# Three always-present slots of split weights in place of four, and three further ones in the MLP in place of two, in a decoder step

## The reference

```
h = rmsnorm(x);  proj = h @ w_in          # 1024 -> 4 x 512: pool channels, q, k, v
A = causal multi-scale pooling of the pool channels, a 128x128 map per group, a gain
B = attention, 8 heads x 64, rotary; decode sequences read 256 paged keys and values
x = x + concat(A, B) @ w_out
x = x + cross_attend(rmsnorm(x), mk, mv, w_cq, w_co)   # 4 heads x 256, 256 memory rows
x = x + square(relu(rmsnorm(x) @ w_up)) @ w_down       # 1024 -> 4096 -> 1024
y = rmsnorm(x)
```

## Time and profile before

| | |
|---|---|
| median of 3 runs | 417.19 us (416.75 to 417.71) |
| the profiled execution's own time | 417.26 us |
| its span in the trace | 415.2 us |
| PE busy | 409.0 us, 99% of the span |
| DVE busy | 253.1 us, 61% |
| ACT busy | 226.7 us, 55% |
| POOL busy | 31.9 us, 8% |
| DMA, mean rate over the span | 233 GB/s |

### The profile page before, as it was taken

The page is one execution under the profiler, slowest core; times in us unless marked ns, Lnnn a source line. Parts: engine busy times, 40 slices in busy tenths (PEclk is TensorE's granted clock), DMA queues, the critical chain, the costliest instruction groups (busy, mean ns, idle before and its releaser), DMA issues.

```text
span 415.2 us, 8425 instructions
## 1 busy us (share of the span) xinstructions
PE 409.0 (99%) x3372; PEld 383.6 (92%) x3372; DVE 253.1 (61%) x400; ACT 226.7 (55%) x392; POOL 31.9 (8%) x41
## 2 busy tenths in 40 slices
PE   8999999999999999999999999999999999999995
PEld 8999979986879998957899999999999999999995
DVE  5899988576254796453259777766667534454302
ACT  5866957925364484424357666666565443453313
POOL 1004026000000120000022000000000000010010
PEclk9999999999999999999999999999999999999999
DMA  8999858974989968995537545655565555545002
GB/s 277 400 385 365 279 205 233 336 275 172 370 313 339 380 228 321 362 394 234 203 103 250 208 135 193 202 181 167 191 202 201 196 174 193 188 162 182 2 2 104
DMA packets 37257, 96.60 MB, mean 233 GB/s; under 512 B 4186, under 2 KB 13274, under 8 KB 37082
## 3 DMA queue, kind: packets, MB, share of 16 engines
q1 hardware_dynamic: 35106, 92.24, 63.5%
q10 hardware_dynamic: 2112, 3.82, 2.5%
HBM read 91.73 MB, written 4.54 MB: 232 GB/s over the span
## 4 chain that ended last, share of the span: by engine, by line
PE 85%; DVE 7%; DMA 4%; SPq 2%; issue 1%; ACT 1%; DVEq 0%
PE psum L1110 70%; PE psum L832 5%; DVE w_lo L1401 2%; PE psum L1052 2%; DMA raw<-in_w_in 2%; PE psum L960 2%; PE psum L947 2%; DMA pages<-in_page_table 1%; DMA raw<-in_w_ck 1%; SPq L778 1%; DVE mix_lo L1405 1%; PE psum L893 1%; PE psum L931 1%; ACT w_hi L1133 1%; PE psum L953 0%
## 5 line engine op out<-in xcount | busy, mean ns | idle before, releaser
L1401 DVE TENSOR_TENSOR w_lo<-raw,w_hi 128x1024 fp32r<-128x1024 f32 x67 | 82.6, 1243 | 61.0 <-ACT w_hi L1133 60.8
L1133 ACT ACTIVATE w_hi<-raw 128x1024 fp32r<-128x1024 f32 (+1 forms) x73 | 73.8, 1019 | 57.8 <-PE psum L1110 41.6
L1110 PE MATMUL psum<-mix_hi,w_hi 128*128 128x264 f32 (+1 forms) x288 | 82.4, 286 | 0.0
L1110 PE MATMUL psum<-mix_hi,w_lo 128*128 128x264 f32 (+1 forms) x288 | 81.1, 282 | 0.0
L1110 PE MATMUL psum<-mix_lo,w_hi 128*128 128x264 f32 (+1 forms) x288 | 81.1, 281 | 0.0
L1110 PE MATMUL psum<-act_hi,w_hi 128*128 128x264 f32 x232 | 66.5, 287 | 0.5 <-DVE w_lo L1401 0.5
L1110 PE MATMUL psum<-act_lo,w_hi 128*128 128x264 f32 x232 | 65.6, 283 | 0.0
L1110 PE MATMUL psum<-act_hi,w_lo 128*128 128x264 f32 x232 | 65.4, 282 | 0.0
L1110 PEld LDWEIGHTS psum<-mix_hi,w_hi 128*128 128x128 f32 x288 | 54.0, 188 | 1.0 <-issue 0.8
L1110 PEld LDWEIGHTS psum<-mix_lo,w_hi 128*128 128x128 f32 x288 | 54.0, 188 | 0.1
L1110 PEld LDWEIGHTS psum<-mix_hi,w_lo 128*128 128x128 f32 x288 | 54.0, 188 | 0.0
(11 more groups left out here) (208 smaller groups left out, 813.9 us busy)
## 6 DMA issues: line engine op xcount, KB each, us to landing
raw<-in_w_down SPq DMA_DIRECT2D x20, 512.0 KB, 3.3
raw<-in_w_up SPq DMA_DIRECT2D x18, 512.0 KB, 3.8
raw_more<-in_w_up SPq DMA_DIRECT2D x14, 512.0 KB, 3.7
stage<-in_mem_v SPq DMA_DIRECT2D x12, 512.0 KB, 6.6
raw_more<-in_w_down SPq DMA_DIRECT2D x12, 512.0 KB, 4.2
stage<-in_cache_v SPq DMA_DIRECT2D x16, 256.0 KB, 6.5
keysT<-in_cache_k SPq DMA_DIRECT2D x16, 256.0 KB, 5.4
keysT<-in_mem_k SPq DMA_DIRECT2D x8, 512.0 KB, 6.9
```

What stands on the lines that cost most here:

```text
L1110: mm = pe.matmul(out, a, b, start=first and m == 0, stop=end_ and m == 2)
L1133: return nc.scalar.activation(out, in_, ACT.Copy, scale=scale)
L1401: V.tensor_tensor(lo_of(c), raw_of(c), hi_of(c).bitcast(F32), ALU.subtract).then_inc(w_lo_ready, 1)
```

## The change

`SPLIT` becomes 3 and `MORE_SPLIT` becomes 3, so that there are six split slots in the MLP as before, and three in place of four up to chunk 55. `AHEAD` follows and becomes 2. Chunk s is then split in turn s-3 until the MLP and waits for chunk s-3. `plan_splits` starts at chunk 3 (`PARTED`), as before in effect: the old start, `AHEAD`, was 3 too. Turn -1, ahead of the loop, has no whole split any more, hence the `.get`: chunk 3 moves into turn 0, chunk 4 into turn 1.

```diff
-SPLIT, MORE_SPLIT = 4, 2
+SPLIT, MORE_SPLIT = 3, 3
 AHEAD = SPLIT - 1
@@ plan_splits
-    for s in range(AHEAD, NC):
+    for s in range(PARTED, NC):
@@ ACT, ahead of its loop
-            for s in SPLITS_AT[0]:
+            for s in SPLITS_AT.get(0, ()):
                 split_hi(s)
```

## The result

The changed kernel takes 422.43 us, the median of four executions (420.7, 422.48, 422.38, 423.3), against 416.97 us for the kernel before on the same chip (four executions, 416.57 to 417.71). The ratio is 1.0124, 95% interval 1.0103 to 1.0144: slower by 1.2%. The forecast was 423.0 us. The profiled execution took 420.7 us, with a span of 418.7 us. The mean granted clock over the span was 1.0 in the profiled execution and 0.948, 0.995 and 0.995 in the three others.

What follows compares the result with a forecast made beforehand. PE's list of matmuls was taken to bound the kernel, busy 409.0 of 415.2 us, so the change could mainly add waits. Six terms summed to 5.8 us on 417.26, giving 423.0 us against the median 417.19; range 419.6 to 427.0.

Steps and rivals of the forecast that it cites:

- Term A: Chunk 4: its low part moves behind the three adds, so PE waits; +1.4 us, between 1.2 and 2.4.
- Terms B and C: Chunks 9 and 13: low parts move behind rotation work; +0.3 us (0 to 1.4) and +0.6 us (0 to 1.6).
- Term D: Prompt scores near 57 us: a moved split may delay DVE emptying their banks; +0.1 us, between -0.2 and +1.1.
- Term E: Chunk 42: split moves behind chunk 39's take-out, and raw loads come later; +2.6 us, between 1.0 and 4.
- the first measure: For each chunk: end of the next chunk's low part before, less the chunk's start on PE before; positive meant lateness.
- rival 1: The loads absorb the shift, joining a backlog and landing when they did; 420.2 us, chance 0.17.
- Term F: From 150 us on: later chunk loads delay decode memory reads sharing SP's queue; +0.8 us, between 0 and 2.2.
- Rival 3: The clock falls to 1.2 GHz behind a wait, one chunk at that level costing 2.9 us; 425.9 us, chance 0.06.
- Rivals 2, 4 and 5: Loads land later and drag PE, 428.2 us, 0.08; nothing changes, 417.2 us, 0.04; faster, 416.5 us, 0.03.

Runs made afterwards that it cites:

- the repeat: The changed kernel run once more, unchanged, for a second trace and more times: 421.01 us, ratio 1.0091.
- five raw slots alone: Changed kernel, three split slots kept, with five raw weight slots from the start in place of three: 418.8 us, ratio 1.004.
- both together: Changed kernel with five raw slots from the start and chunk 4's split put back in its old place: 417.32 us, ratio 1.0014.
- the late places: Kernel before, four and two split slots kept, with splits at the changed kernel's places, one turn later: 418.68 us, ratio 1.0053.
- late loads: Kernel before, four split slots and old split places; loads of chunks 36 to 44 wait for one chunk later's low part: 422.63 us, ratio 1.0124.
- the pair of kernels: Kernel before with loads of chunks 36 to 44 delayed, without and with 20 spare matmuls before chunk 42: 422.63 and 420.57 us.

## Why the prediction was right, and where it was not

The sign and the mechanism held: three slots make PE later at the four chunks named, and nothing changes in the MLP. But that 423.0 us came close to 422.43 us was in good part luck: two errors offset each other. The terms come to 3.4 us in place of 5.8, and the clock, which was a rival, most likely added some 1.5 us to three of the four executions, and late landings some tenths. In the repeat, where one of five executions was of this kind, the median was 421.01 us. For two of the three the mean granted clock of 0.995 says so, the same as in the traced fall of the repeat. The third has 0.948, which would be some 44 us at the lower level (an estimate: 0.052 of 420.4 us, doubled) in an execution that took no longer than the others; this stays unexplained. A trace with the fall was taken of one execution of this kernel only, in the repeat.

**Term A** was right to 0.1 us, and for the reason given: low part 4 ended 0.1 us before the time worked out (18.92 against 19.05). Putting that split back under loads that do not hold it up saves some 1.4 us (five raw slots alone are 1.9 us over the kernel before on the same chip, both together 0.5).

**Terms B and C** were right: +0.15 and +0.70 for 0.3 and 0.6. They are all that remains with both large causes taken away (+0.5 us, interval 0.2 to 1.0). At chunk 9 PE's lateness grows without a marked wait.

**Term D** had the wrong sign. PE does not wait for the bank any more, and the time between chunk 13 and there became 0.44 us shorter, of which the old wait was 0.2. That is outside the range, whose lower end was -0.2. Of the further 0.24 us, 0.18 are gained at the matmuls of L884, at 53.03 us before; the cause was not looked into.

**Term E** is the step that failed in size, +1.6 for +2.6, and its two parts failed differently. The first, 1.0 us for the place of split 42 alone, rested on moving everything around the take-out with PE. The run of the late places with four slots shows 0 there. In the kernel before, DVE's adds were held up by low parts 41 and 42, and those by a landing, and the change takes low part 42 out of their way; so this stretch had room against PE that the first measure, the end of low part s+1 less the start of chunk s, does not see. It sees where a low part ended, not what it had waited for. The second part, the late raw loads, was right in kind. High part 41 came at 144.73 us, where the prediction had 146 for itself and 143.5 for rival 1; it is nearly half way. That the whole step is 1.6 us, as this part was to be, is chance. By the prediction's own count this part is how much more the adds are late than PE: 3.7 - 2.2 there, 2.26 - 1.63 here, 0.6 us. The other 1.0 is the place of split 42 after all, but it costs only where late loads hold the take-out back. The prediction's 2.2 us for PE's lateness ahead of chunk 42 is also not its own sum of A to D, which is 2.4. That the loads are the cause is shown from both sides: five raw slots remove the wait (421.01 to 418.8), and late loads with four split slots make it (417.25 to 422.63). The terms also are not independent. With PE 1.3 us less late the wait grew by 0.7, so that undoing A alone saved 0.9 us (421.01 to 420.14) rather than 1.3.

**Term F** was not there: no wait for a landing near 188 us, and PE's lateness goes from 3.33 at chunk 42 to 3.44 us at the end. PE had fallen as far behind as the loads.

**The rivals.** Rival 1 gave 420.2 us for loads that absorb the shift. In the executions where the clock holds, 420.7 us, the truth lies nearer to it than to the forecast. Rival 3 was given 6% and makes most of the rest. The prediction put against it that the longest wait is 2.6 us; but a wait of 2.14 us was followed by 0.50. Its price in that trace is 1.5 us and not the 2.9 us of one chunk at the lower level, since the stretch ends within the chunk. The executions of 422.4 to 423.3 us lie 1.7 to 2.6 us over the others; later landings may be part of that. With late loads the lower level lasted longer: PE lost 2.7 us from the second wait's end to its last matmul, and the pair of kernels differs by 2.1 us in the median. The Trainium skill (TensorE: Matmul & The Clock Gate, "What's actually happening"), which the prediction named for the fall and the return of the clock, agrees with these traces in kind: 0.50 behind a wait, 1.00 again with PE busy. Rivals 2, 4 and 5 are out: no term reached its upper bound, the waits came, and nothing was won. The waits of PE came to 4.2 us where the prediction looked for about 7.5.

What stays open is what decides whether the clock falls in a given execution. With a wait of 1.53 us and one of 2.23 us it stayed at 1.00; behind one of 2.14 us it fell. In the kernel of the late places alone, two of six executions took 420.2 and 420.4 us against 418.6, without such a wait in the profiled one and with mean granted clocks of 0.997 and 0.998; their cause was not found either.

## What to carry to other kernels

Fewer buffers in a chain of stages cost where something else stands in the written order between two uses, and through the stage that feeds it: here the loss at the far end of the attention came from raw slots being released later, and more raw slots cured it. Before a shift is priced by where an instruction ended, look at what it had waited for: a stretch that itself waits for a landing has room against the engine that seems to set it. A wait of some 2 us in front of a busy TensorE can have a second price behind it, in some executions and not in others. Independent matmuls in the wait took it away with late loads; in the changed kernel no execution with them was slow, but the median was no lower.

## What the runs showed of the hardware

The granted clock fell to 0.50 at waits that the prediction had thought too short to matter: 2.14 us in one execution, and 1.51 and 1.44 us with six matmuls between them in another. PE had been fully busy up to the first wait in both. The stretches ahead of it, in the repeat of the changed kernel and in the kernel with late loads (columns as before):

```profile
141.00:151.00 10.00, 10.00 (x86) 10.00 (x85) 6.61 (x11) 5.04 (x10) 1.79 (x3) 1.00 0.98 374
```

```profile
130.00:148.80 18.80, 18.80 (x158) 18.68 (x156) 10.20 (x15) 7.75 (x14) 2.33 (x3) 1.00 0.83 307
```

The lower level lasted 3.4 us in the first and 6.8 us in the second. With 20 spare matmuls before chunk 42 in the kernel with late loads it did not come in the profiled execution, and the median time fell by 2.1 us.
